# Gate pieces moved from the first steps of one attention into the last steps of the one before it

## The chip, the cores and the metric

The kernel runs on one core of one Trainium2 chip. The metric is the device time of one execution, in microseconds; the number given is the median of several runs.

## The reference

Two transformer layers in sequence, on 512 rows of 1024 columns, all in 32-bit floats. The change lies in the second layer, whose mixing part is, cut to what matters:

```python
h = rms_norm(x, g_mix)
proj = h @ w_in
sb_q, sb_k, sb_v, d_q, d_k, d_v, m_q = jnp.split(proj, IN_SPLITS, axis=-1)
y_sb = stick_breaking_attention(...) @ w_o_sb      # 8 heads, no softmax: a reverse cumulative sum
y_dil = dilated_mixture(...) @ w_o_dil             # 3 groups of 4 heads, dilations 1, 4, 16
y_mem = memory_attention(...) @ w_o_mem            # 4 heads over 256 memory rows
gates = jax.nn.sigmoid(h @ w_gate + b_gate)        # 3 x 1024 columns
merged = gates[0] * y_sb + gates[1] * y_dil + gates[2] * y_mem
x = x + merged @ w_out
```

The product `h @ w_gate` needs only `h`, so it can be made at any time before `merged`.

## The kernel before

The kernel is one program of several blocks. In a block each of the five engines has its own instruction list, and waits for the others through semaphores, which count up; `e.wait_ge(*s(n))` waits for the n-th increment of s. At the end of a block all engines drain and meet at a barrier. Nothing of the next block starts before.

Two blocks matter here. The **first** (line 2260) is the stick-breaking attention with the projections of the dilated attention beside it. It is written as a pipeline over 41 steps: in step n, PE makes the scores of unit n (a head and a block of 128 queries), transposes the weights of unit n-5, multiplies the values of unit n-7, and so on; ACT (ScalarE) and DVE (VectorE) do their parts of other units (`pe_stick`, `act_stick`, `dve_stick`). The projections (`pe_jobs`) end with step 27.

The **second** (line 2461) is the dilated attention (`att_d`, 48 units, one a step) with the heads of the memory attention beside it. Its first steps prepare these: from step 2 to step 8 DVE squares, sums and scales six tiles of queries and keys (`dve_memory`; `dve_newton`, line 282, begins with the first operation of each norm's Newton step), with two small operations on ACT between (lines 274 and 276); PE transposes each from step 4 on (line 2382). The tiles come from DRAM, loaded by SP at the start of this block (line 2466), behind a load of 1.5 MB of gate weights (`load_early`, line 1590).

The **gate pieces** are filler for PE. Of the product `h @ w_gate` (transposed, 24 units of 128 gate columns and all 512 rows), 12 units are made early, in 96 pieces. A piece (`pe_early(e, p)`, lines 1603 to 1615) is a unit s = p // 8 and a slice k = p % 8 of the inner dimension, in three matmuls of 128x512, since a 32-bit product is made of a high and a low part of each side. For unit s:

- ACT rounds the weights to the high part (`act_early`, line 1596), DVE subtracts to get the low part (`dve_early`, line 1601). The two are called a split below. Unit s needs its split before its first piece.
- The result goes to bank `EB[s]` of PSUM: 4, 5, 4, 7, 6, 7 for units 0 to 5.
- When the eighth piece is done, DVE (first block, line 2306) or ACT (`act_early_out`, line 2421) copies the bank to a buffer, and SP stores it to DRAM (`store_early`, line 1624).

In the first block the splits of units 0 to 4 stand at steps 27, 29, 31, 35 and 39 (`EARLY_AT`). PE makes two pieces in each of the steps 28 to 39, 24 in all, so units 0, 1 and 2. DVE copies them out at steps 32, 36 and 40. In the second block the list `FILL` says how many pieces PE makes in each step, ahead of that step's attention. Two tables follow from it: `SPLITS` (the step of each further split: one step after unit s-3 has ended) and `OUTS` (the step of ACT's copy: one step after the unit has ended). In the order of a step, ACT makes its split and its copy first, then its part of the memory heads and of the attention; DVE makes its split last.

Of the kernel before, what the change touches and what calls it, by code (L numbers as in the profile page):

```python
# [176 lines left out]
def r(a):  # L177
    return a.bitcast(F32R)


def span(k, w=128):
    return slice(w * k, w * k + w)


def program(nc, d, out, sizes):
    ctx = ExitStack()
    with ctx:
# [29 lines left out]
        def sems(names, new=False):  # L217
            return [sem(n, new) for n in names.split()]
# [981 lines left out]
        with ExitStack() as c0:  # L1200
# [359 lines left out]
            def load_job(e, t):  # L1560

                if t >= 26:
                    e.wait_ge(*j_mm(4 * (t - 26) + 4))
                e.dma_start(JW[t % 2][0][:, 0:sizes[t]], w_src(t)).then_inc(*w_in[t % NS].up(16))
# [24 lines left out]
            def load_early(e, g):  # L1589
                e.dma_start(ER[g % 2][0].rearrange("p k n -> p (k n)"), w_src(31 + 2 * g)).then_inc(*er_in[g % 2].up(16))  # L1590
# [12 lines left out]
            def pe_early(e, p):  # L1603
                s, k = divmod(p, 8)
                g, b = divmod(s, 3)
                bk, hi, lo = bank[EB[s]], EH[:, k, span(b)], ER[g % 2][1][:, k, span(b)]
                if k == 0:
                    e.wait_ge(*e_lo(s + 1))
                    if early_prior(s) >= 0:
                        e.wait_ge(*e_out(early_prior(s) + 1))  # L1610
                e.matmul(bk, r(lo), r(HTh[:, k, :]), start=k == 0, stop=False)
                e.matmul(bk, r(hi), r(HTl[:, k, :]), start=False, stop=False)
                i = e.matmul(bk, r(hi), r(HTh[:, k, :]), start=False, stop=k == 7)
                if k == 7:
                    i.then_inc(*e_mm.up(1))
# [351 lines left out]
        with ExitStack() as c0:  # L1967
# [34 lines left out]
            with ExitStack() as c1:  # L2002
# [21 lines left out]
                j_sq, j_out, j_var, j_root, j_norm, j_turn, j_keep, j_cols, j_odd = sems("j_sq j_out j_var j_root j_norm j_turn j_keep j_cols j_odd")  # L2024
# [231 lines left out]
                        e.tensor_scalar(va_[n % 2], ss, 1.0 / 64, EPS, ALU.mult, ALU.add).then_inc(*j_var.up(1))  # L2256

                EARLY_AT = (27, 29, 31, 35, 39)

                with nc.Block() as block:  # L2260
                    @block.sync
                    def _(e):
                        e.wait_ge(*mq_done(64))
                        for t in range(26, 31):
                            load_job(e, t)
                        e.wait_ge(*j_turn(16))
                        e.wait_ge(*j_var(16))
                        e.dma_start(BD, d["bd"]).then_inc(*bd_in.up(16))
                        e.wait_ge(*j_mm(24))
                        load_early(e, 0)  # L2270
                        e.wait_ge(*j_mm(28))
                        load_early(e, 1)
                        for s in range(3):
                            store_early(e, s)

                    @block.tensor
                    def _(e):
                        for step in range(41):
                            pe_stick(e, step)
                            pe_jobs(e, step)  # L2280
                            if 28 <= step < 40:
                                if step in (28, 32):
                                    e.wait_ge(*j_out(27 + (step - 28) // 4))
                                for p in range(2 * step - 56, 2 * step - 54):
                                    pe_early(e, p)

                    @block.scalar
                    def _(e):
                        exp_and_ln(e)
                        for step in range(42):  # L2290
                            if step in EARLY_AT:
                                act_early(e, EARLY_AT.index(step))
                            act_stick(e, step)
                            act_jobs(e, step)

                    @block.vector
                    def _(e):
                        for step in range(41):
                            dve_stick(e, step)
                            dve_jobs(e, step)  # L2300
                            if step in EARLY_AT:
                                dve_early(e, EARLY_AT.index(step))
                            if step in (32, 36, 40):
                                s = (step - 32) // 4
                                wait_early_out(e, s)
                                e.tensor_copy(ZG[s % 2], bank[EB[s]]).then_inc(*e_out.up(1))

# [3 lines left out]
            with ExitStack() as c1:  # L2311
# [51 lines left out]
                STEPS = att_d.steps()  # L2363

                FILL = [2] * 10 + [1] * 4 + ([0] * 2 + [1] * 8) * 2 + [0] * 6 + [1] * (STEPS - 40)
                filled = [24 + int(x) for x in np.cumsum([0] + FILL)]
                ended = lambda s: next((step for step in range(STEPS) if filled[step + 1] >= 8 * s + 8), STEPS)
                split_at = lambda s: max(0, ended(s - 3) + 1) if s > 5 else 0  # L2370
                SPLITS, OUTS = {split_at(s): s for s in range(5, 12)}, {ended(s) + 1: s for s in range(3, 12) if ended(s) < STEPS}
# [1152 lines left out]
```

## Time and profile before

| what | before |
|---|---|
| runs, us | 2824.06, 2825.64, 2825.81 (median 2825.64) |
| profiled execution, us | 2824.89 |
| its span, us | 2823.1 |
| busy us: PE, DVE, ACT, POOL | 2753.9, 2015.8, 1380.0, 441.9 |
| mean granted clock of TensorE | 0.992 |
| first block, us from the span's start | about 1060 to 1249 |
| second block | about 1250 to 1385 |

Times in the rows are microseconds from the start of the span. PE is TensorE's matmuls, PEld its weight loads, DVE is VectorE, ACT ScalarE, SP the engine that issues most DMAs; a q behind the name is the engine's queue (drains, semaphores, DMA issues). A bracket behind a row gives the idle time before it and what ended it. Ends of matmuls are modelled; from start to start is the surer measure. Granted clock 1.00 is 2.4 GHz, 0.50 is 1.2 GHz.

### The profile page before, as it was taken

The page shows a single profiled execution, that of the slowest core. Times are in us where ns is not written, and L with a number is a line of the kernel's source. Part 1 is how long each engine was busy: PE and PEld are TensorE (multiplying, and loading weights), DVE is VectorE, ACT ScalarE, POOL GpSimd, SP SyncE. Part 2 cuts the span into 40 slices and gives each one's busy share as a digit, 9 for nine tenths or more (in the row PEclk, how much of TensorE's full clock was granted, in tenths as well). Part 3 has the DMA queues.
Part 4 walks back from the last instruction along what each step waited for, and adds up shares of the span by engine and source line. Part 5 has one row for each costly group of instructions (what it writes and reads, how often), then busy time and mean ns, then how long its engine had stood idle before and what let it go on. Part 6 is the DMA issues. An engine that isn't in the chain of part 4 may idle for free. (4 is left out here: it accounts for less than half of the span.)

```text
span 2823.1 us, 36694 instructions
## 1 busy us (share of the span) xinstructions
PE 2753.9 (98%) x13927; PEld 2344.3 (83%) x13927; DVE 2015.8 (71%) x3290; ACT 1380.0 (49%) x2203; POOL 441.9 (16%) x294
## 2 busy tenths in 40 slices
PE   8989999999999899989999999999999999999999
PEld 6756888688888689968788889999999988888887
DVE  5575533688888616775654787788788868888886
ACT  4336522477777516665432433466667733333332
POOL 0000000010100000000000000222224424454442
PEclk9999999999999999999999999999999999999999
DMA  5000262667776521121242424777889989999996
GB/s 197 29 24 1 90 172 99 269 238 303 279 305 254 221 81 64 68 85 39 96 141 96 160 97 144 236 261 279 295 280 337 361 313 390 385 388 395 391 387 258
DMA packets 166623, 600.48 MB, mean 213 GB/s; under 512 B 16048, under 2 KB 87472, under 8 KB 138288
## 3 DMA queue, kind: packets, MB, share of 16 engines
q1 hardware_dynamic: 107696, 436.08, 42.3%
q0 software_dynamic: 41472, 138.45, 13.1%
q10 hardware_dynamic: 17280, 23.60, 2.3%
q8 instruction: 112, 1.84, 0.3%
q14 instruction: 63, 0.52, 0.1%
HBM read 563.96 MB, written 71.86 MB: 225 GB/s over the span
## 5 line engine op out<-in xcount | busy, mean ns | idle before, releaser
L2893 POOL DMA_INDIRECT RG<-in_un,EI x128 | 200.9, 1569 | 1155.7 <-DVE EI L3163 824.6
L2893 POOL DMA_INDIRECT RG<-in_vn,EI x128 | 198.2, 1548 | 276.5 <-DVE X L2907 253.4
L3288 PE MATMUL bank<-VH,GL 128*128 128x512 f32 x768 | 208.0, 392 | 0.4 <-DVE GL L2959 0.4
L3284 PE MATMUL bank<-VH,GH 128*128 128x512 f32 x768 | 207.9, 392 | 0.0
L2907 DVE SCALAR_TENSOR_TENSOR X<-RG,DG,X 128x1024 f32<-128x1024 f32 x128 | 164.1, 1282 | 53.3 <-DMA RG<-in_vn,EI 50.9
L2874 PE MATMUL bank<-HTl,UHe 128*128 128x384 f32 x512 | 175.2, 342 | 0.0
L2874 PE MATMUL bank<-HTl,UH1r 128*128 128x384 f32 x512 | 174.6, 341 | 0.0
L3288 PEld LDWEIGHTS bank<-VH,GL 128*128 128x128 f32 x768 | 144.1, 188 | 33.3 <-DVE GL L2959 0.9
L2875 PE MATMUL bank<-HTh,UHe 128*128 128x384 f32 x512 | 171.4, 335 | 0.0
L2875 PE MATMUL bank<-HTh,UH1r 128*128 128x384 f32 x512 | 171.3, 335 | 0.0
L3284 PEld LDWEIGHTS bank<-VH,GH 128*128 128x128 f32 x768 | 144.2, 188 | 32.5
L2904 DVE CUSTOM_DVE_ANT_0 RG<-RG,HR 128x1024 f32<-128x1024 f32 x128 | 156.5, 1222 | 16.2 <-DMA RG<-in_un,EI 15.4
L2966 ACT ACTIVATE VH<-VR 128x2048 fp32r<-128x2048 f32 x64 | 119.6, 1909 | 93.3 <-DMA VR<-in_vn 93.3
L3262 ACT ACTIVATE GA<-bank 128x384 f32<-128x384 f32 x120 | 58.3, 486 | 164.3 <-PE bank L2878 161.4
L3200 ACT ACTIVATE OAB<-OAB,IA 128x128 f32<-128x128 f32 x384 | 122.2, 392 | 16.9 <-DVE OAB L3193 16.0
L3193 DVE TENSOR_TENSOR OAB<-C,IA 128x1024 f32<-128x1024 f32 x96 | 116.9, 1221 | 1.6 <-PE bank L3208 1.5
L3292 PE MATMUL bank<-VR0r,GH 128*128 128x512 f32 x384 | 105.3, 396 | 0.2 <-DVE VR0r L2971 0.2
L3292 PE MATMUL bank<-VR1r,GH 128*128 128x512 f32 x384 | 102.9, 390 | 0.2 <-DVE VR1r L2971 0.2
L3208 PE MATMUL bank<-OAB 128*128 128x128 f32 x768 | 98.4, 275 | 2.0 <-ACT OAB L3200 2.0
L3208 PEld LDWEIGHTS bank<-OAB 128*128 128x128 f32 x768 | 96.4, 191 | 2.4 <-ACT OAB L3200 2.4
L2874 PEld LDWEIGHTS bank<-HTl,UHe 128*128 128x128 f32 x512 | 96.3, 188 | 0.8 <-DVE HTl L3440 0.5
L2874 PEld LDWEIGHTS bank<-HTl,UH1r 128*128 128x128 f32 x512 | 96.3, 188 | 0.2
(749 smaller groups left out, 7589.5 us busy)
## 6 DMA issues: line engine op xcount, KB each, us to landing
VR<-in_vn SPq DMA_DIRECT2D x32, 2048.0 KB
UP<-in_wup SPq DMA_DIRECT2D x22, 2048.0 KB, 7.6
UR<-in_u SPq DMA_DIRECT2D x42, 1024.0 KB
DN<-in_wdn SPq DMA_DIRECT2D x32, 1024.0 KB, 7.4
wspill<-VR SPq DMA_DIRECT2D x12, 2048.0 KB
aspill<-GA ACTq DMA_DIRECT2D x120, 192.0 KB
URew<-in_u SPq DMA_DIRECT2D x22, 1024.0 KB
W<-in_weights SPq DMA_DIRECT2D x10, 2048.0 KB, 9.3
```

Source lines behind the costliest of these rows:

```text
L2874: e.matmul(bk, r(hi[:, k, :]), r(HL_[:, k, 0:NT3]), start=k == 0, stop=False)
L2875: e.matmul(bk, r(hi[:, k, :]), r(HH_[:, k, 0:NT3]), start=False, stop=False)
L2893: e.indirect_dma_start(RG[q % RR], None, d["un" if what == "u" else "vn"][:, :], off).then_inc(*row_in[q % RR].up(16))
L2904: e.tensor_tensor_reduce(RG[q % RR], RG[q % RR], HR3, 1.0, 0.0, ALU.mult, ALU.add, DT[:, s:s + 1]).then_inc(*r_used.up(1))
L2907: e.scalar_tensor_tensor(X[:, 3, :], RG[q % RR], DG[:, s:s + 1], X[:, 3, :], ALU.mult, ALU.add).then_inc(*r_used.up(1))
L2966: e.activation(r(VH[n % 3]), VR[g % 2][0][:, :, span(n % 2, 512)], ACT.Copy).then_inc(*v_hi.up(1))
L3193: e.tensor_tensor(OAB[n % 3], cc("iota").unsqueeze(1).unsqueeze(1).to_broadcast(to), IA[:, 0:2, span(n, 4)].unsqueeze(3).to_broadcast(to), ...
L3200: i = e.activation(OB[n % 3][:, j, :], OB[n % 3][:, j, :], ACT.Copy, scale=IA[:, 2, t:t + 1])
L3208: i = e.matmul(bank[2 + n % 3][:, span(j)], OA[n % 3][:, j, :], OB[n % 3][:, j, :], start=True, stop=True)
L3284: e.matmul(bk, r(gh[:, a, t]), r(vh[:, a, :]), start=g == 0 and a == 0, stop=False)
L3288: e.matmul(bk, r(gl[:, a, t]), r(vh[:, a, :]), start=False, stop=False)
L3292: i = e.matmul(bk, r(gh[:, a, t]), r(vl[:, a, :]), start=False, stop=g == 31 and a == 3)
```

## The change

The first block's pieces are now given by a table: two in each of the steps 28 to 35, three in each of 36 to 39, four in step 40; 32 in all, so units 0 to 3. DVE copies unit 2 out at step 39 where it was 40. In the second block the first eight steps have one piece each where they had two; from step 8 on it is as before, piece for piece. All 96 pieces are made, with the same banks.

```diff
--- before.py
+++ after.py
@@ -2256,6 +2256,7 @@
                         e.tensor_scalar(va_[n % 2], ss, 1.0 / 64, EPS, ALU.mult, ALU.add).then_inc(*j_var.up(1))
 
                 EARLY_AT = (27, 29, 31, 35, 39)
+                PIECES = [int(x) for x in np.cumsum([0] * 29 + [2] * 8 + [3] * 4 + [4])]
 
                 with nc.Block() as block:
                     @block.sync
@@ -2278,11 +2279,10 @@
                         for step in range(41):
                             pe_stick(e, step)
                             pe_jobs(e, step)
-                            if 28 <= step < 40:
-                                if step in (28, 32):
-                                    e.wait_ge(*j_out(27 + (step - 28) // 4))
-                                for p in range(2 * step - 56, 2 * step - 54):
-                                    pe_early(e, p)
+                            if step in (28, 32):
+                                e.wait_ge(*j_out(27 + (step - 28) // 4))
+                            for p in range(PIECES[step], PIECES[step + 1]):
+                                pe_early(e, p)
 
                     @block.scalar
                     def _(e):
@@ -2300,8 +2300,8 @@
                             dve_jobs(e, step)
                             if step in EARLY_AT:
                                 dve_early(e, EARLY_AT.index(step))
-                            if step in (32, 36, 40):
-                                s = (step - 32) // 4
+                            if step in (32, 36, 39):
+                                s = (step - 31) // 4
                                 wait_early_out(e, s)
                                 e.tensor_copy(ZG[s % 2], bank[EB[s]]).then_inc(*e_out.up(1))
 
@@ -2364,8 +2364,8 @@
 
 
 
-                FILL = [2] * 10 + [1] * 4 + ([0] * 2 + [1] * 8) * 2 + [0] * 6 + [1] * (STEPS - 40)
-                filled = [24 + int(x) for x in np.cumsum([0] + FILL)]
+                FILL = [1] * 8 + [2] * 2 + [1] * 4 + ([0] * 2 + [1] * 8) * 2 + [0] * 6 + [1] * (STEPS - 40)
+                filled = [PIECES[-1] + int(x) for x in np.cumsum([0] + FILL)]
                 ended = lambda s: next((step for step in range(STEPS) if filled[step + 1] >= 8 * s + 8), STEPS)
                 split_at = lambda s: max(0, ended(s - 3) + 1) if s > 5 else 0
                 SPLITS, OUTS = {split_at(s): s for s in range(5, 12)}, {ended(s) + 1: s for s in range(3, 12) if ended(s) < STEPS}
```

`SPLITS` and `OUTS` are worked out from the new list. Since unit 3 now ends in the first block, the split of unit 6 and the copy of unit 3 move from step 4 to step 1; the others stay.

PE's list at the end of the first block and the start of the second, before (lines 1611 to 1613 are the three matmuls of a piece; bank 4 is unit 2, bank 7 unit 3; line 438 is a score of the dilated attention):

```order
L1611 MATMUL bank4<-Xr_49,ER0l_5188 128x512
L1612 MATMUL bank4<-HTr_50,EH_5191 128x512
L1613 MATMUL bank4<-Xr_49,EH_5191 128x512
L2260 UNCONDITIONAL_BRANCH
L2481 UNCONDITIONAL_BRANCH
L1611 MATMUL bank7<-Xr_49,ER1l_5190 128x512
L1612 MATMUL bank7<-HTr_50,EH_5191 128x512
L1613 MATMUL bank7<-Xr_49,EH_5191 128x512
L1611 MATMUL bank7<-Xr_49,ER1l_5190 128x512
L1612 MATMUL bank7<-HTr_50,EH_5191 128x512
L1613 MATMUL bank7<-Xr_49,EH_5191 128x512
L438 MATMUL bank0<-dkT,dqT 128x128
```

and with the change (bank 6 is unit 4):

```order
L1611 MATMUL bank7<-Xr_49,ER1l_5190 128x512
L1612 MATMUL bank7<-HTr_50,EH_5191 128x512
L1613 MATMUL bank7<-Xr_49,EH_5191 128x512
L2261 UNCONDITIONAL_BRANCH
L2481 UNCONDITIONAL_BRANCH
L1611 MATMUL bank6<-Xr_49,ER1l_5190 128x512
L1612 MATMUL bank6<-HTr_50,EH_5191 128x512
L1613 MATMUL bank6<-Xr_49,EH_5191 128x512
L438 MATMUL bank0<-dkT,dqT 128x128
L1611 MATMUL bank6<-Xr_49,ER1l_5190 128x512
L1612 MATMUL bank6<-HTr_50,EH_5191 128x512
L1613 MATMUL bank6<-Xr_49,EH_5191 128x512
```

The first block now ends with pieces of unit 3, and between its start and the first score the second block has one piece of unit 4 instead of two of unit 3.

ACT's list at the start of the second block, before (line 271 loads the activation table, 1596 is ACT's half of a split, 500 the exponential of an attention unit, 2421 a copy of a finished gate unit, 2396 a copy of a transposed memory tile):

```order
L271 ACT_TABLE_LOAD
L1596 ACTIVATE EH<-ER1w 128x8x128
L500 ACTIVATE Pd,RSd<-Pd,NMd 128x128
L274 ACTIVATE rtm<-vam 128x4
L276 ACTIVATE rtm<-rtm 128x4
L500 ACTIVATE Pd,RSd<-Pd,NMd 128x128
L274 ACTIVATE rtm<-vam 128x4
L276 ACTIVATE rtm<-rtm 128x4
L500 ACTIVATE Pd,RSd<-Pd,NMd 128x128
L1596 ACTIVATE EH<-ER0w 128x8x128
L2421 ACTIVATE ZG_5193<-bank 128x512
```

and with the change:

```order
L271 ACT_TABLE_LOAD
L1596 ACTIVATE EH<-ER1w 128x8x128
L1596 ACTIVATE EH<-ER0w 128x8x128
L2421 ACTIVATE ZG_5193<-bank 128x512
L500 ACTIVATE Pd,RSd<-Pd,NMd 128x128
L274 ACTIVATE rtm<-vam 128x4
L276 ACTIVATE rtm<-rtm 128x4
L500 ACTIVATE Pd,RSd<-Pd,NMd 128x128
L274 ACTIVATE rtm<-vam 128x4
L276 ACTIVATE rtm<-rtm 128x4
L500 ACTIVATE Pd,RSd<-Pd,NMd 128x128
```

The split of unit 6 (from ER0w) and the copy of unit 3 now stand ahead of the first exponential, where they stood behind the third. On DVE the other half of that split has moved in the same way, ahead of the first norm:

```order
 L470 ISA Pd,NMd<-bank,BD 128x128
 L470 ISA NMd 128x1
+L1601 TENSOR_TENSOR ER0l<-ER0w,EH 128x8x128
 L1991 TENSOR_TENSOR oTm<-oTm 128x512
 L1993 TENSOR_REDUCE ssm<-oTm 128x4
```

Line 470 is the reduction of an attention unit's scores, 1991 the first operation of a norm. SP's list is the same.

## Rows read from the trace of the kernel before

**Rows 1.** The page: its first line and the busy time of PE.

```profile
span 2823.1 us, 36694 instructions
...
PE 2753.9 (98%) x13927; PEld 2344.3 (83%) x13927; DVE 2015.8 (71%) x3290; ACT 1380.0 (49%) x2203; POOL 441.9 (16%) x294
```

**Rows 2.** Timeline of PE, end of the first block, start of the second (start us, us, what).

```profile
1245.46 0.40 PE L1611 MATMUL bank<-Xr,ER0l 128*128 128x512 f32 x1
...
1246.16 0.60 PE L2048 MATMUL bank<-C,oTm 128*128 128x128 f32 x4
...
1247.76 0.40 PE L1613 MATMUL bank<-Xr,EH 128*128 128x512 f32 x1
...
1249.68 0.47 PE L1611 MATMUL bank<-Xr,ER1l 128*128 128x512 f32 x1 [1.52 <-PEq L2260]
```

**Rows 3.** Windows: busy us of each engine, then granted clock, DMA share, GB/s.

```profile
1240.00:1248.20 8.20, 8.16 (x48) 6.63 (x46) 2.75 (x5) 3.58 (x5) 0.00 (x0) 1.00 0.09 34
```

**Rows 4.** Drains at the first block's end, line 2260 (durations ns, start us).

```profile
L2260 DVEq DRAIN  x1: 725/725/725, 1248.2 to 1248.2; - x1
...
L2260 SPq DRAIN  x1: 124/124/124, 1249.3 to 1249.3; - x1
```

**Rows 5.** The same for PE at the barrier of line 681.

```profile
L681 PEldq DRAIN  x1: 5332/5332/5332, 219.2 to 219.2; - x1
```

**Rows 6.** Timeline of PE behind that barrier.

```profile
224.84 1.10 PE L438 MATMUL bank<-kbT,qbT 128*128 128x512 f32 x2 [0.30 <-PEq L681]
```

**Rows 7.** Timeline of DVE, second block, steps 0 to 7.

```profile
1252.10 1.22 DVE L1601 TENSOR_TENSOR ER1l<-ER1w,EH 128x1024 fp32r<-128x1024 f32 x1 [3.21 <-ACT EH L1596]
...
1257.12 0.69 DVE L1991 TENSOR_TENSOR oTm<-oTm 128x512 f32<-128x512 f32 x1 [3.59 <-DMA oTm<-mqs]
...
1259.25 0.16 DVE L282 TENSOR_TENSOR thm<-rtm 128x4 f32<-128x4 f32 x1 [0.31 <-ACT rtm L276]
...
1262.96 0.16 DVE L282 TENSOR_TENSOR thm<-rtm 128x4 f32<-128x4 f32 x1 [0.31 <-ACT rtm L276]
...
1266.34 1.22 DVE L1601 TENSOR_TENSOR ER0l<-ER0w,EH 128x1024 fp32r<-128x1024 f32 x1
1267.47 0.15 DVE L282 TENSOR_TENSOR thm<-rtm 128x4 f32<-128x4 f32 x1
...
1271.18 0.16 DVE L282 TENSOR_TENSOR thm<-rtm 128x4 f32<-128x4 f32 x1
...
1278.01 0.29 DVE L461 COPY PTd<-bank 128x128 f32<-128x128 f32 x1
```

**Rows 8.** Timeline of SP's queue behind the barrier: the load for unit 6.

```profile
1249.63 0.33 SPq L1590 DMA_DIRECT2D ER0w<-in_weights  x1
```

**Rows 9.** DMA issues, window 1245 to 1262: KB, us to landing.

```profile
ER0w<-in_weights SPq DMA_DIRECT2D x1, 1536.0 KB, 6.8
```

**Rows 10.** Timeline of PE, second block: two waits, and a slow piece's start and follower.

```profile
1258.99 0.80 PE L438 MATMUL bank<-dkT,dqT 128*128 128x128 f32 x2 [3.53 <-DVE NMd L470]
...
1260.87 0.63 PE L1611 MATMUL bank<-Xr,ER1l 128*128 128x512 f32 x1
...
1262.15 0.41 PE L431 MATMUL bank<-C,Pd 128*128 128x128 f32 x1
...
1278.45 0.41 PE L431 MATMUL bank<-C,Pd 128*128 128x128 f32 x2 [0.60 <-DVE PTd L461]
```

**Rows 11.** Timeline of ACT, second block: a split's half and a copy.

```profile
1250.94 1.06 ACT L1596 ACTIVATE EH<-ER1w 128x1024 fp32r<-128x1024 f32 x1
...
1264.17 0.57 ACT L2421 ACTIVATE ZG<-bank 128x512 f32<-128x512 f32 x1
```

**Rows 12.** Windows, columns as in rows 3.

```profile
1234.00:1237.40 3.40, 2.02 (x15) 1.54 (x14) 3.21 (x4) 3.36 (x4) 0.00 (x0) 1.00 0.00 0
...
1259.00:1263.30 4.30, 4.16 (x12) 3.06 (x12) 3.40 (x12) 1.37 (x8) 0.00 (x0) 0.50 0.05 21
1263.30:1267.50 4.20, 3.44 (x14) 2.69 (x14) 3.92 (x11) 2.97 (x9) 0.00 (x0) 0.77 0.24 62
```

## The prediction

> **What bounds the kernel now.** I read the page first: TensorE (PE) is busy for 98% of a span of 2823.1 us [rows 1], so nearly every stretch is paced by PE, and the question is whether the places the change touches are among the exceptions. They are two blocks: the stick-breaking attention (steps 0 to 40) and, behind a barrier of all engines, the dilated attention with the memory heads.
>
> Next, PE's timeline at the end of the first block. From step 28 on each step carries two gate pieces, of three 128x512 matmuls each. There a piece costs 0.70 us from start to start (1245.46 to 1246.16 [rows 2]), and over steps 36 to 39 PE has no idle time: it is busy for 8.16 of 8.20 us [rows 3]. So those steps are PE's own, and whatever is added there is paid in full. Then comes the barrier: PE's last matmul ends at 1248.16 and the first of the next block starts at 1249.68, 1.52 us later [rows 2]. The rows of the drains say why. When PE is done, DVE is still copying unit 2 out of its bank until 1248.9; SP then issues the store of that copy and is drained at 1249.4 [rows 4], 0.3 us before PE's start. So it is the chain PE, DVE copy, SP store that ends the block. Where PE was itself the last to arrive, at the barrier of line 681 (drain of 5.33 us from 219.2, so to 224.5), it was idle for 0.30 us only [rows 5, 6].
>
> Third, DVE in the second block's first steps. At step 2 it wants the first memory queries from DMA and gets them at 1257.12, 7.49 us after SP's first issue at 1249.63 [rows 7, 8]. From there on it works through six norms, one a step. The starts of the first operation of the Newton step (line 282) are at 1259.25, 1262.96, 1267.47 and 1271.18, so 3.71, 4.51 and 3.71 us apart [rows 7], and two more follow in the last rhythm. The one longer step is the one with the split of unit 6 in it (1.22 us, line 1601). A period that stays at 3.71 us, at TensorE's half clock as at its full one, and whether the attention's tiles have 128 or 256 columns, has no PE in it: it is DVE's chain with ACT's two small operations between. PE waits for it: 3.53 us at 1258.99, and again at 1278.45 for the copy that DVE starts at 1278.01 [rows 7, 10]. Behind 1278.45 PE hardly waits any more; from step 8 on it is the bound again.
>
> **The change, part by part.**
>
> *Eight pieces more in the first block* (one each in steps 36 to 39, four in step 40). PE has no idle time to put them in: 8 x 0.70 = +5.60 us. No new wait: the weights of unit 3 are split in step 35 as before, and its bank 7 is free, since PE's product in step 38 already waits for the copy of the bank's last transposes.
>
> *The copy of unit 2 one step sooner.* Unit 2 now ends with the second piece of step 38; copy and store run beside the following pieces, six of them, 4.2 us against 0.69 us of copy and the 0.5 us to SP's drain. The barrier then waits for PE alone. I take the 0.30 us of the barrier where PE came last; the other bound is that the gap stays at 1.52. So 0.30 - 1.52 = -1.22 us, with 0 as the other end. The second block's first matmul starts 5.60 - 1.22 = 4.38 us later.
>
> *Eight pieces fewer in steps 0 to 7 of the second block.* 8 x 0.70 = 5.60 us of PE work go, at least. In steps 0 to 2 PE then reaches the wait for DVE sooner and waits longer. In steps 3 to 7 DVE's 3.71 us is the period, and PE is idle more. I cost it at 0. The cover is DVE's chain; were PE the pace in steps 3 to 7, five pieces would be worth 3.5 us, and that is the bound on this side.
>
> *Split and copy moved forward.* Since unit 3 now ends in the first block, ACT's split of unit 6 (line 1596) and its copy of unit 3 (line 2421) go from step 4 to step 1, and DVE's half of the split too. This adds a wait: ACT stands at step 1 until the weights have landed. SP issues them behind the barrier, as before, and they land 6.8 us later [rows 9]. Queued behind on ACT: the copy and the first exponential. Queued behind on DVE: step 2, the first norm. From the barrier: 6.8 landing + 1.06 ACT's half [rows 11] + 0.10 from its end to DVE's start (1252.00 to 1252.10 [rows 7, 11]) + 1.13 DVE's half (1266.34 to 1267.47 [rows 7]) = 9.09 us, where DVE started its norm at 7.49. That is +1.60 us. ACT's exponential comes after 6.8 + 1.06 + 0.57 [rows 11], at 8.4; PE asks for its result only behind its third scores, and these wait for a reduction that DVE makes behind the norm at 9.1, so it delays nothing. In return step 4 loses its split: 4.51 - 3.71 = -0.80 us. Net +0.80. Bounds: 0 (the weights land sooner and the queries are last again; then even -0.80) and +1.60 (step 4 does not get shorter).
>
> The Trainium skill has a formula for this landing (DMA: Bandwidth & Descriptors, "Anatomy of one DMA", there for transfers issued by GpSimd): 2.0 us and the bytes at 436 GB/s, which for 1.57 MB would be 5.6 us. By that the split would delay DVE by 1.2 us less and the sum would be 4.0; the trace's 6.8 us decides.
>
> *Sum:* 5.60 - 1.22 + 0 + 0.80 = **+5.2 us**. The profiled execution took 2824.89 us, its span and 1.8 us around it; with the sum 2830.1. It lies 0.75 below the median of the three runs (2825.64), to which I add the same: **2830.8 us**. Everything behind the second block sits behind further barriers and only shifts. About 0.2%, or 5.65 us, is what a measurement of this kernel can tell from no change; the forecast is just inside it.
>
> **The rivals.**
>
> *The clock stays low (slower).* PE's wait now spans some 6 us instead of 3.5. After the 3.5 us TensorE's granted clock fell to its lower level, 1.2 GHz, and stayed there throughout 1259.0 to 1263.3 though PE was busy for 4.16 of 4.30 us, and for some 1.9 of the next 4.20 us (mean 0.77) [rows 12]: 6.2 us in all. With one piece a step PE is less busy afterwards, and if it were still at 1.2 GHz when it becomes the bound in steps 8 and 9, another stretch of 6.2 us there would cost half of itself, 3.1 us: +8.3, 2833.9 us. It decides from the point where the low clock reaches beyond DVE's last norm. Against it: at the low clock a piece takes 1.28 us (1260.87 to 1262.15 [rows 10]), so PE is busy nearly all of the 3.71 us and should return to full speed; and a stretch with PE busy for 2.02 of 3.40 us kept a clock of 1.00 [rows 12]. The Trainium skill (TensorE: Matmul & The Clock Gate, Part 1) says that idling halves the clock and sustained work gives it back, and advises against gaps such as this change lengthens; by that rule too the low stretch begins during the wait, which DVE's chain covers. Chance 0.15.
>
> *The gap at the barrier does not close.* PE's gap was 1.52 us here, and no row shows it closing with a DMA store just finished. Then +6.4, 2832.0 us. For it: only one barrier shows the 0.30. Against it: its rows name DVE and SP as the late ones. Chance 0.14.
>
> *The removed pieces were on the path.* If PE is the pace in steps 3 to 7: 5.2 - 3.5 = +1.7, 2827.3 us. For it: PE is busy most of these steps, and waits there are short. Against it: the constant 3.71. Chance 0.15.
>
> *Something not seen makes it faster by over 0.2%.* All of PE's work is still there, and even with the last rival and the split at its lower end of -0.8 the sum is 5.60 - 1.22 - 3.5 - 0.8 = +0.1. Chance 0.06.
>
> **How the numbers follow.** My case has 0.50; its spread is about 1 us, so 0.38 of it lies within 0.2% and 0.12 above. Same: 0.38 + 0.15 = 0.53. Slower: 0.12 + 0.15 + 0.14 = 0.41. Faster: 0.06. The range reaches from a little under the third rival, 2826.0, to a little over the first, 2834.5; outside remain the 0.06 and the tails of both.
>
> **What would show each step.** In the changed profile: the last piece of the first block ends 5.6 us later with no idle time before it, and PE's idle time over the barrier is 0.3 us; DVE's first norm starts 9.1 us behind SP's first issue, released by ACT's split and not by DMA; PE's wait before the third scores grows from 3.5 to about 6 us; all five periods of line 282 are 3.7 us; the granted clock is 1.00 again before the last norm. I am wrong if these periods shrink (PE was the pace), if the low clock reaches into the steps with two pieces, or if the gap stays 1.5 us.

## The result, and the profile after

| | before | with the change |
|---|---|---|
| median of 12 runs, us | 2825.72 | 2829.93 |
| lowest to highest | 2821.02 to 2831.22 | 2827.48 to 2833.49 |
| ratio, 95% interval | | 1.0017 [1.0009, 1.0024] |
| span of the profiled execution | 2823.1 | 2830.3 |

The change makes the kernel slower by 0.17%, 4.8 us by the ratio and 4.2 by the medians; 5.2 was forecast. A second sample of the same kernel (experiment e12) gave 1.0016 [1.0008, 1.0025].

The page of the changed kernel hardly differs; compare [rows 1]. The number of instructions is the same, and PE has the same work (the share falls from 98% to 97%) in a longer span.

```profile
span 2830.3 us, 36694 instructions
...
PE 2755.3 (97%) x13927; PEld 2343.9 (83%) x13927; DVE 2016.1 (71%) x3290; ACT 1380.4 (49%) x2203; POOL 440.9 (16%) x294
```

The spans of the two profiles differ by 7.2 us, more than the kernels do. So first cut the time where it can be cut without doubt, at the barriers. In both profiles the barriers' semaphore rows give the time from one to the next; these are the blocks that matter here, with the ones around them:

| from barrier to barrier, us | before | after | after again (e12) |
|---|---|---|---|
| four blocks up to the first block | 1060.4 | 1062.0 | 1062.1 |
| first block | 189.2 | 193.5 | 193.5 |
| second block | 135.8 | 136.3 | 136.2 |
| third block | 173.8 | 173.8 | 175.4 |
| last block | 1263.8 | 1264.6 | 1264.3 |

The rows are printed to 0.1 us, so a difference can be 0.1 us off. In the 14 profiles of this study the first two blocks repeat to 0.2 us for the same instructions, with one exception (the first block of e1, below); the others wander by 2 to 4 us from profile to profile, whatever the kernel. So the change is +4.3 and +0.5 us, and the rest of the 7.2 is not its own.

**The end of the first block**, timeline of PE, to be laid beside [rows 2] and [rows 10]:

```profile
1241.67 0.48 PE L1611 MATMUL bank<-Xr,ER0l 128*128 128x512 f32 x1
...
1254.84 0.40 PE L1613 MATMUL bank<-Xr,EH 128*128 128x512 f32 x1
1255.56 0.47 PE L1611 MATMUL bank<-Xr,ER1l 128*128 128x512 f32 x1 [0.32 <-PEq L2261]
...
1259.47 0.62 PE L438 MATMUL bank<-dkT,W 128*128 128x128 f32 x2 [2.06 <-DVE NMd L470]
...
1266.22 0.80 PE L438 MATMUL bank<-dkT,dqT 128*128 128x128 f32 x2 [4.85 <-DVE NMd L470]
...
1288.34 0.60 PE L438 MATMUL bank<-dkT,dqT 128*128 128x256 f32 x2
```

The columns are start and duration in us, and in brackets the idle time before it and what ended it. From step 36's first piece (here 1241.67; before 1240.12) to the last matmul's end it takes 13.57 us where it took 8.04 us: +5.53 for eight pieces. There is no idle time in it, and the gap over the barrier is 0.32 us, where [rows 2] had 1.52. The drains say who came last, beside [rows 4]; DVE's copy is over at 1250.0, SP is drained at 1250.5, PE at 1255.3:

```profile
L2261 DVEq DRAIN  x1: 725/725/725, 1249.3 to 1249.3; - x1
L2261 SPq DRAIN  x1: 124/124/124, 1250.4 to 1250.4; - x1
...
L2261 PEldq DRAIN  x1: 4352/4352/4352, 1250.9 to 1250.9; - x1
```

**The start of the second block**, SP's first issue, its landing, and ACT, beside [rows 8], [rows 9] and [rows 11]:

```profile
1255.52 0.33 SPq L1590 DMA_DIRECT2D ER0w<-in_weights  x1
```

```profile
ER0w<-in_weights SPq DMA_DIRECT2D x1, 1536.0 KB, 6.6
```

```profile
1262.12 1.06 ACT L1596 ACTIVATE EH<-ER0w 128x1024 fp32r<-128x1024 f32 x1 [4.25 <-DMA ER0w<-in_weights]
1263.09 0.58 ACT L2421 ACTIVATE ZG<-bank 128x512 f32<-128x512 f32 x1
1263.56 0.39 ACT L500 ACTIVATE Pd<-Pd,NMd 128x128 f32<-128x128 f32 x1
```

ACT stands idle for 4.25 us for the weights, and the first exponential, behind split and copy, starts 8.04 us after SP's first issue.

**DVE's chain of norms**, beside [rows 7]:

```profile
1263.21 1.23 DVE L1601 TENSOR_TENSOR ER0l<-ER0w,EH 128x1024 fp32r<-128x1024 f32 x1 [3.80 <-ACT EH L1596]
1264.35 0.68 DVE L1991 TENSOR_TENSOR oTm<-oTm 128x512 f32<-128x512 f32 x1
...
1266.47 0.16 DVE L282 TENSOR_TENSOR thm<-rtm 128x4 f32<-128x4 f32 x1 [0.31 <-ACT rtm L276]
...
1270.18 0.16 DVE L282 TENSOR_TENSOR thm<-rtm 128x4 f32<-128x4 f32 x1 [0.31 <-ACT rtm L276]
...
1273.90 0.16 DVE L282 TENSOR_TENSOR thm<-rtm 128x4 f32<-128x4 f32 x1 [0.26 <-ACT rtm L276]
...
1277.61 0.16 DVE L282 TENSOR_TENSOR thm<-rtm 128x4 f32<-128x4 f32 x1
```

The first norm (1264.35) starts behind the split and not behind a DMA, 8.83 us after the issue; it was 7.49. The periods of line 282 are 3.71, 3.72 and 3.71 us: the 4.51 us one is gone. PE's ninth scores come at 1288.34, 32.82 us behind the issue at 1255.52; before it was 1281.90 behind 1249.63, 32.27 us (timeline of PE in the kernel before):

```profile
1281.90 0.60 PE L438 MATMUL bank<-dkT,dqT 128*128 128x256 f32 x2
```

So the way from DVE's first norm to the ninth scores takes 24.78 us before (1257.12 to 1281.90) and 23.99 us with the change (1264.35 to 1288.34): 0.79 us less, which is what the step lost with its split, and nothing for the eight pieces that are gone. The rest of the difference is the start of the chain, 8.83 against 7.49 us. From the third scores to the last of the block both profiles agree step by step to 0.05 us, but for the step that lost its split: 4.16 us before, 3.38 after.

**TensorE's clock**, windows (busy us of PE, PEld, DVE, ACT, POOL, then granted clock, DMA share, GB/s), beside [rows 3] and [rows 12]; first the whole low stretch of the kernel before, then the changed kernel:

```profile
1258.40:1265.20 6.80, 6.07 (x18) 4.78 (x19) 5.60 (x20) 3.48 (x11) 0.00 (x0) 0.50 0.11 45
```

```profile
1241.70:1255.20 13.50, 13.50 (x70) 11.07 (x68) 3.29 (x5) 3.43 (x5) 0.00 (x0) 1.00 0.11 40
...
1260.50:1266.20 5.70, 0.87 (x3) 0.14 (x1) 2.88 (x6) 2.12 (x5) 0.00 (x0) 0.50 0.77 303
1266.20:1273.20 7.00, 5.22 (x15) 3.60 (x15) 5.82 (x17) 2.08 (x9) 0.00 (x0) 0.50 0.06 16
1273.20:1277.50 4.30, 2.10 (x13) 1.79 (x13) 3.71 (x13) 1.98 (x8) 0.00 (x0) 0.98 0.33 75
```

The lower clock now lasts nearly 14 us (1259.7 to 1273.3) instead of nearly 7, and ends well ahead of the last norm at 1285. In the second profile of the same kernel (e12) it lasted 17 us, and the second block took no longer for it (136.2 us).

### The profile page after: what moved, and what is told of

Read it like the earlier page. It is cut to its first block and busy times, and to the rows that moved or that the text cites. A ratio compares the mean times of both kernels' runs of the same rounds, so it can differ in the third digit from the quotient of the medians.

```text
span 2830.3 us, 36694 instructions
## 1 busy us (share of the span) xinstructions
PE 2755.3 (97%) x13927; PEld 2343.9 (83%) x13927; DVE 2016.1 (71%) x3290; ACT 1380.4 (49%) x2203; POOL 440.9 (16%) x294
## 5 line engine op out<-in xcount | busy, mean ns | idle before, releaser
L2875 PEld LDWEIGHTS bank<-HTh,UHe 128*128 128x128 f32 x512 | 96.3, 188 | 0.2
```

The lines of the kernel that those rows point to most:

```text
L2875: e.matmul(bk, r(hi[:, k, :]), r(HH_[:, k, 0:NT3]), start=False, stop=False)
```

## The experiments

All edits are to the kernel named, and each kernel was timed beside the kernel before on the same chip. The ratios have intervals of about 0.09% to either side, 2.5 us, so that a difference of 1 us is read from the time between barriers, and only the sum from the ratio.

**e1: is it the early split that delays DVE?** In the changed kernel, split and copy back at step 4.

```diff
-split_at = lambda s: max(0, ended(s - 3) + 1) if s > 5 else 0
+split_at = lambda s: 4 if s == 6 else max(0, ended(s - 3) + 1) if s > 5 else 0
-OUTS = {ended(s) + 1: s for s in range(3, 12) if ended(s) < STEPS}
+OUTS = {(4 if s == 3 else ended(s) + 1): s for s in range(3, 12) if ended(s) < STEPS}
```

> The changed kernel, but unit 6's split and unit 3's copy stand at step 4 of the second block again. My theory (DVE's chain paces the steps 2 to 8, and the early split delays its start): DVE's first norm is released by the queries' DMA, 7.1 to 7.5 us behind SP's first issue instead of 8.8; the period of line 282 with the split in it is 4.5 us again, the others 3.7; PE's wait before the third scores is some 3.5 us instead of 4.85; from barrier to ninth scores the time is 0.4 to 0.7 us less than in the changed kernel (32.8 us). Rival (the delay is of the low clock or of the missing pieces, not of the split): the time from barrier to ninth scores stays at 32.8 us.

One execution, 2831.25 us; timeline of DVE:

```profile
1262.52 0.69 DVE L1991 TENSOR_TENSOR oTm<-oTm 128x512 f32<-128x512 f32 x1 [3.32 <-DMA oTm<-mqs]
...
1268.35 0.16 DVE L282 TENSOR_TENSOR thm<-rtm 128x4 f32<-128x4 f32 x1 [0.31 <-ACT rtm L276]
...
1271.72 1.22 DVE L1601 TENSOR_TENSOR ER0l<-ER0w,EH 128x1024 fp32r<-128x1024 f32 x1
1272.86 0.15 DVE L282 TENSOR_TENSOR thm<-rtm 128x4 f32<-128x4 f32 x1
```

The first norm waits for the DMA again, 7.21 us behind SP's issue at 1255.31; the period with the split in it (1268.35 to 1272.86) is 4.51 us; the second block takes 135.5 us instead of 136.3. The ninth scores come 0.85 us sooner than in the changed kernel, a little more than the 0.4 to 0.7 expected, since the queries landed sooner than in the kernel before (7.21 us and not 7.49). From the first norm to the ninth scores it takes 24.76 us, as before. The clock was low for as long as in the changed kernel, so it is the split that cost the half microsecond, not the clock.

This one profile is the exception among the first blocks: 195.0 us, 1.5 more than in the changed kernel, whose instructions it has there. A stretch of low clock fell just behind the barrier (the changed kernel has a clock of 1.00 there), and PE is busy in it:

```profile
1061.20:1064.50 3.30, 3.30 (x12) 3.30 (x12) 0.00 (x0) 0.38 (x1) 0.00 (x0) 0.50 0.01 2
```

**e2: is PE's work in the first eight steps free?** The kernel before, with all but the last matmul of units 3 and 4 left out: 46 of 48 matmuls of steps 0 to 7. Two of the twelve early gate units are then not what they should be.

```diff
 def pe_early(e, p):
...
+    if s in (3, 4) and k < 7:
+        return
...
+    if s in (3, 4):
+        e.matmul(bk, r(hi), r(HTh[:, k, :]), start=True, stop=True).then_inc(*e_mm.up(1))
+        return
```

> The kernel before, with units 3 and 4 of the gates left out but for one matmul each (46 of 48 matmuls, 10.7 us of PE work at full clock, of the first eight steps of the second block). My theory: PE's work in these steps is free, so leaving it out brings nothing: periods of line 282 stay 3.7 us (4.5 with the split), the ninth scores come within 0.3 us of the 32.3 us behind the barrier that they have in the kernel before, the total is within 1 us (ratio 0.9997 to 1.0004). Rival (the removed pieces were on the path): 3.5 us or more faster, ratio 0.9988 or less. Rival (low clock): PE is idle so much that the clock stays at 1.2 GHz into steps 8 and 9, and the total is 2 to 4 us longer, ratio 1.0007 to 1.0014.

Timeline of DVE, then windows:

```profile
1258.22 0.16 DVE L282 TENSOR_TENSOR thm<-rtm 128x4 f32<-128x4 f32 x1 [0.31 <-ACT rtm L276]
...
1261.94 0.16 DVE L282 TENSOR_TENSOR thm<-rtm 128x4 f32<-128x4 f32 x1 [0.31 <-ACT rtm L276]
...
1266.44 0.16 DVE L282 TENSOR_TENSOR thm<-rtm 128x4 f32<-128x4 f32 x1
...
1270.15 0.16 DVE L282 TENSOR_TENSOR thm<-rtm 128x4 f32<-128x4 f32 x1
```

```profile
1250.20:1277.50 27.30, 11.99 (x41) 9.21 (x42) 20.47 (x60) 10.45 (x33) 0.00 (x0) 0.50 0.38 138
1277.50:1284.00 6.50, 6.27 (x39) 5.40 (x40) 4.25 (x15) 5.03 (x14) 0.00 (x0) 0.98 0.11 40
```

3.72, 4.50 and 3.71 us: with nearly 11 us of PE work gone, the chain keeps its time. The second block took 135.7 us (before 135.8). This is the plainest sign that DVE's chain is the pace. The clock was low for 27 us, up to 1277.7, 3 us ahead of the ninth scores at 1280.86, and cost nothing either: from the first norm to the ninth scores it takes 24.76 us (before 24.78).

But the median was 2827.75 us, ratio 1.0018 [1.0009, 1.0027]: slower. The profile shows none of it in the two blocks; but the profiled execution took 2824.23 us, the second shortest of the twelve and less than the profiled one of the kernel before, so it can't show where the others lost their time. Two more runs asked why. **e9** has the same partial sums as e2 with all instructions in place (the last matmul of units 3 and 4 has `start=True`, so begins the sum anew):

```diff
-    e.matmul(bk, r(hi), r(HTl[:, k, :]), start=False, stop=False)
-    i = e.matmul(bk, r(hi), r(HTh[:, k, :]), start=False, stop=k == 7)
+    e.matmul(bk, r(hi), r(HTl[:, k, :]), start=False, stop=s in (3, 4) and k == 7)
+    i = e.matmul(bk, r(hi), r(HTh[:, k, :]), start=s in (3, 4) and k == 7, stop=k == 7)
```

> The kernel before, instruction for instruction, but the last matmul of units 3 and 4 begins its sum anew, so that these two units hold the same partial product as in e2 and only the data behind them differ. It asks why e2 took 4 us more in the median while its two blocks took none more. Theory A (the data: other gates, so other experts are chosen and other rows gathered later): the same ratio as e2, 1.0009 to 1.0027. Theory B (the missing matmuls, through the low clock or the layout of the program): 0.9995 to 1.0005.

It gave 1.0003 [0.9994, 1.0012], so the data alone hardly do it, though this interval still overlaps both of the other kernel's. **e10** is e2 once more:

> e2 once more (units 3 and 4 left out but for one matmul each), since its two blocks took no longer in the profile than before while its median was 4 us above, and e9 with the same data was not. If that was a sampling matter: ratio 0.9997 to 1.0007. If the missing work makes it slower: 1.0009 or more again, and a profile of a slow execution should show a low granted clock that reaches behind DVE's last norm, into steps 8 and later.

It gave 1.0011 [1.0002, 1.0019], with 189.1 and 135.5 us in the two blocks, and again a low clock of 27 us that ended with the last norm (at 1280.5). The expected low clock in steps 8 and later is not there; the profiled execution took 2826.91 us, again less than its sample's median (2827.97). The slowness repeats and no profile shows its place. The granted clocks of the single executions give a hint: their mean is 0.9879 and 0.9878 in the two samples, where the kernel before, timed beside them, had 0.9925 and 0.9923. That is some 26 us more at the lower level, and the second block, with 27 us instead of nearly 7, accounts for 20 of them. The 5 or 6 us left, at half price where PE is busy, would be an estimated 3 us of the 3 to 5. It is not shown; the cause stays open. What e2 was made for, the two blocks, is clear in both of its profiles.

**e3: does it matter where the pieces are taken from?** The changed kernel's 32 pieces in the first block, but taken out of steps 8 to 13, where PE is the bound.

```diff
-FILL = [1] * 8 + [2] * 2 + [1] * 4 + ([0] * 2 + [1] * 8) * 2 + [0] * 6 + [1] * (STEPS - 40)
+FILL = [2] * 8 + [0] * 6 + ([0] * 2 + [1] * 8) * 2 + [0] * 6 + [1] * (STEPS - 40)
```

> The changed kernel's first block (32 pieces), with two pieces in each of the second block's first eight steps as in the kernel before, and none in steps 8 to 13 (where before had two, two and four times one): the eight pieces are taken out where PE is the bound. My theory: 5.5 us dearer in the first block, 1.2 less at the barrier, 0.5 more for the early split, and up to 5.6 less in steps 8 to 13, as far as these steps have no other bound: total -0.7 to +1.5 us against before (ratio 0.9997 to 1.0005), so 4 to 5 us faster than the change. Rival (pieces are worth the same wherever they are taken out, and the change's cost comes from the block's end or from the split): the same total as the change, ratio 1.0017.

Ratio 1.0013 [1.0004, 1.0023], which alone would not part the two. The barriers do: first block 193.4 us, as in the change, second 133.1, which is 3.2 less than in the change and 2.7 less than before. The split of unit 6 stands at step 1 as in the change, but step 4 keeps one, that of unit 7, so the chain starts late (8.7 us) and saves nothing: 24.77 us to the ninth scores. From there to the fifteenth it took 10.94 us instead of 14.88: eight pieces of 0.70 gave 3.9 us and not 5.6, since with its filler gone PE waits for others (timeline of PE in e3):

```profile
1285.74 0.41 PE L431 MATMUL bank<-C,Pd 128*128 128x128 f32 x2 [1.65 <-issue]
...
1290.03 0.70 PE L438 MATMUL bank<-KV,mqT 128*128 128x256 f32 x2 [0.24 <-ACT PM L500]
```

So my figure for this place was too high by 1.7 us, and in sum the two blocks cost +1.5 us, the upper end of the -0.7 to +1.5 expected; the ratio came out above its forecast (0.9997 to 1.0005). The order of size holds: 0 for pieces out of DVE's steps, 3.9 us out of PE's.

**e4: what starts the chain?** The kernel before, with two query tiles loaded ahead of unit 6's weights.

```diff
 e.wait_ge(*e_mm(3))
+for tb in range(2):
+    e.dma_start(MS[tb], d["mqs"][span(tb), :]).then_inc(*mq_in[tb].up(16))
 load_early(e, 2)
-for tb in range(4):
+for tb in range(2, 4):
     e.dma_start(MS[tb], d["mqs"][span(tb), :]).then_inc(*mq_in[tb].up(16))
```

> The kernel before, with SP loading the first two query tiles ahead of unit 6's weights. My theory: DVE's chain of norms paces PE from the third scores to the ninth, and it starts when the first tile lands. It lands 2 to 2.6 us behind the barrier instead of 7.5, DVE is then ready 3.9 us behind the barrier (behind its split of unit 5 and the first reduction), so the chain starts 3.5 us sooner, PE's wait of 3.5 us before the third scores falls to nearly nothing, the clock stays at 2.4 GHz, the ninth scores come 3 to 3.6 us sooner and the total is 3 to 3.6 us shorter (ratio 0.9987 to 0.9990). Rival (PE is the pace once it does not wait): 0 to 1.5 us.

Timeline of DVE in e4:

```profile
1254.61 0.69 DVE L1991 TENSOR_TENSOR oTm<-oTm 128x512 f32<-128x512 f32 x1
...
1256.73 0.16 DVE L282 TENSOR_TENSOR thm<-rtm 128x4 f32<-128x4 f32 x1 [0.31 <-ACT rtm L276]
...
1260.44 0.16 DVE L282 TENSOR_TENSOR thm<-rtm 128x4 f32<-128x4 f32 x1 [0.31 <-ACT rtm L276]
...
1264.96 0.15 DVE L282 TENSOR_TENSOR thm<-rtm 128x4 f32<-128x4 f32 x1
```

The norm starts 3.82 us behind SP's first issue (1250.79) and waits for no DMA; the chain keeps its periods (3.71, 4.52); the ninth scores come 28.59 us behind the issue, 3.7 us sooner. Ratio 0.9991 [0.9982, 0.9999], 2.5 us. Of the 3.7 us the block kept 2.3 (133.6 us), since in this profile a stretch of low clock (1348.6 to 1352.0) fell in the steps without filler, 34 to 39, and the last three of these took 1.3 us longer than before. The rival's 0 to 1.5 us is out for the ninth scores.

**e5, e6, e7: the same reasons used for a better kernel.** e5 is e4 with the splits of units 6 and 7 at steps 9 and 11. e6 adds a piece in each of steps 2 to 5 and takes four out of steps 8 to 13. e7 adds the end of the first block as in the change, with two extra pieces only.

```diff
+split_at = lambda s: {6: 9, 7: 11}.get(s, max(0, ended(s - 3) + 1) if s > 5 else 0)      # e5, e6, e7
+FILL = [2, 2, 3, 3, 3, 3, 2, 2] + [1] * 4 + [0] * 2 + ([0] * 2 + ...                     # e6
+FILL = [2, 2, 3, 3, 3, 3, 2, 2] + [0] * 2 + [1] * 2 + [0] * 2 + ([0] * 2 + ...           # e7
+PIECES = [int(x) for x in np.cumsum([0] * 29 + [2] * 8 + [3, 3, 2, 1, 1])]               # e7, e8
-for p in range(2 * step - 56, 2 * step - 54):
+for p in range(PIECES[step], PIECES[step + 1]):                                          # e7, e8
-if step in (32, 36, 40):
+if step in (32, 36, 39):                                                                 # e7, e8
```

> The kernel before with the queries loaded first (as e4) and the splits of units 6 and 7 at steps 9 and 11 of the second block instead of 4 and 8. My theory (DVE's chain of norms is the pace up to the ninth scores): all five periods of line 282 are 3.7 us, the ninth scores come 0.8 us sooner than in e4 (28.6 us behind SP's first issue; e4 had 28.6 at 29.4 with its own split), total 4 to 5 us shorter than before, ratio 0.9983 to 0.9987. Rival (PE paces these steps once it does not wait): no gain over e4's 2.5 us.

> As e5, and four pieces more in steps 2 to 5 of the second block (three each), four fewer in steps 8 to 13. My theory: the four cost nothing where DVE's chain paces (period stays 3.7 to 3.8 us; PE's work of a step is then just under 3.7), and 2 to 2.8 us go from steps 8 to 13, where PE is the bound and e3 gained 3.9 us by eight pieces: total 6 to 7.5 us shorter than before, ratio 0.9973 to 0.9979. Rival (a piece costs its 0.7 us wherever it stands): the same as e5.

> As e6, and the first block's end as in the change, but with two pieces of unit 3 only (26 in all; unit 2 ends at step 38, its copy at step 39), taken out of steps 8 and 9. My theory: 1.4 us more before the barrier, 1.2 less at it (PE's gap 0.3 us), 0.7 to 1.4 less in steps 8 and 9: 0.5 to 1.2 us shorter than e6, ratio to before 0.9969 to 0.9977. Rival (the barrier's gap is not closed by two pieces, 1.8 us of PE work against 1.2 of copy and store): 0 to 1 us longer than e6.

> e7 once more, to narrow its interval. Its first two blocks together took 6.6 us less than before in the profile, and a third block with one more stretch at the low clock gave 1.6 us of it back. Expected ratio 0.9976 to 0.9986; if the low clock behind it is systematic 0.9982, else 0.9977.

DVE's chain in e5:

```profile
1252.91 0.69 DVE L1991 TENSOR_TENSOR oTm<-oTm 128x512 f32<-128x512 f32 x1
...
1255.04 0.16 DVE L282 TENSOR_TENSOR thm<-rtm 128x4 f32<-128x4 f32 x1 [0.31 <-ACT rtm L276]
...
1258.75 0.16 DVE L282 TENSOR_TENSOR thm<-rtm 128x4 f32<-128x4 f32 x1 [0.31 <-ACT rtm L276]
...
1262.47 0.16 DVE L282 TENSOR_TENSOR thm<-rtm 128x4 f32<-128x4 f32 x1 [0.26 <-ACT rtm L276]
...
1266.19 0.16 DVE L282 TENSOR_TENSOR thm<-rtm 128x4 f32<-128x4 f32 x1
```

All periods are 3.71 or 3.72 us now, and the ninth scores come 27.37 us behind the issue, 1.2 us sooner than in e4 (step 8 lost a split too). But the splits cost something where they went, at steps 9 and 11, behind the chain of norms: from the ninth scores to the fifteenth it takes 15.78 us, where it took 14.88. Of the 1.2 us, 0.3 are left.

| | first block | second block | third block | ratio to before |
|---|---|---|---|---|
| before | 189.2 | 135.8 | 173.8 | |
| e4 | 189.1 | 133.6 | 175.3 | 0.9991 [0.9982, 0.9999] |
| e5 | 189.1 | 131.9 | 177.0 | 0.9993 [0.9985, 1.0002] |
| e6 | 189.1 | 129.8 | 175.4 | 0.9984 [0.9974, 0.9994] |
| e7 | 189.3 | 129.1 | 175.4 | 0.9986 [0.9976, 0.9997] |
| e7 again (e11) | 189.3 | 129.1 | 173.8 | 0.9966 [0.9954, 0.9978] |

The second block shrinks at each step: 1.7 us from e4 to e5 (1.3 of them only because e4's profile had its stretch of low clock in steps 37 to 39; 0.3 are the splits'), 2.1 from e5 to e6 (three pieces a step did not stretch DVE's period: it is 3.72 in e6 too), 0.7 from e6 to e7, in whose first block the two pieces and the closed gap nearly cancel (+0.2). In all 6.6 us go from the two blocks (189.2 + 135.8 to 189.3 + 129.1). The ratios missed their forecasts: e5, e6 and the first e7 came out higher (0.9983 to 0.9987, 0.9973 to 0.9979 and 0.9969 to 0.9977 were forecast), e7's second sample lower (0.9976 to 0.9986). That e5's is no better than e4's fits the 0.3 us. The forecasts for e6 and e7 fit what the two blocks lost, 6.1 us (0.9978) and 6.6 us (0.9977), and these values lie within the measured intervals, so that the ratios alone can't say whether something was lost elsewhere. e7 beats both kernels in both of its samples, and the two samples' intervals hardly meet.

**e8: the barrier alone.** Kernel before, with e7's `PIECES`, copy of unit 2 at step 39, two pieces fewer in steps 8 and 9, splits kept where they were.

```diff
+FILL = [2] * 8 + [1] * 6 + ([0] * 2 + ...
+split_at = lambda s: {6: 4, 7: 8}.get(s, max(0, ended(s - 3) + 1) if s > 5 else 0)
```

> The kernel before with the barrier part of the change alone: 26 pieces in the first block (3, 3, 2, 1, 1 in steps 36 to 40), copy of unit 2 at step 39, and the two pieces taken out of steps 8 and 9 of the second block; splits of units 6 and 7 kept at steps 4 and 8, queries as before. My theory: first block 0.1 to 0.3 us longer (+1.4 for two pieces, -1.2 at the barrier, PE's gap 0.3 us), second block 0.7 to 1.4 shorter: 0.5 to 1.3 us shorter in all, which only the profile can show; ratio 0.9994 to 1.0001. Rival (the gap stays 1.5 us): first block 1.4 us longer.

Timeline of PE in e8, first matmul behind the barrier:

```profile
1247.36 0.47 PE L1611 MATMUL bank<-Xr,ER1l 128*128 128x512 f32 x1 [0.30 <-PEq L2261]
```

The gap closes with two pieces (1.4 us) behind unit 2's end as well as with the change's eight (5.6 us). First block 189.3 us, second 134.3; ratio 0.9997 [0.9988, 1.0005]. The second block's 1.6 us are a little more than the 0.7 to 1.4 expected: 0.4 of them came from queries that landed sooner (first norm 7.10 us behind the issue, not 7.49).

**e12: the change again.**

> The changed kernel once more beside these. My theory: +4.3 us from the first block and +0.5 from the second in every execution, ratio 1.0012 to 1.0022; first block 193.5 us from barrier to barrier, second 136.3, as in its first profile, and any other difference of a profile lies outside these two. Rival (the agreement of the first profile was luck): the second block differs from 136.3 by over 1 us.

1.0016 [1.0008, 1.0025], with 193.5 and 136.2 us: as the first time. From the first norm to the ninth scores it takes 23.99 us again.

## Why the prediction was right

- *Eight pieces at full price in the first block.* Forecast +5.60, measured +5.53 us, with PE busy for 13.50 of 13.50 us. Right.
- *The gap at the barrier closes.* Forecast -1.22 from one row of another barrier; measured 1.52 to 0.32, so -1.20. The rival that it stays open is out; e8 closes it too. The prediction counted six pieces (4.2 us) behind unit 2's end; they are eight, the whole of unit 3 (5.6 us), which makes the cover larger and changes no term.
- *Fewer pieces in steps 0 to 7 bring nothing.* Forecast 0, since the 3.71 us period did not move with the clock or the tile width. Right: after the change it is still 3.71, and e2 takes out twice as much PE work and it is still 3.71. From the first norm to the ninth scores it takes 24.76 to 24.79 us in the kernel before and in e1, e2 (both profiles), e3, e4 and e9, with two pieces a step, one, or hardly any PE work, and 23.99 us in both profiles of the change, without the split. The rival worth 3.5 us is out.
- *Split moved forward.* Forecast +1.60 for DVE's start and -0.80 at step 4; measured +1.34 (the weights landed after 6.6 us, not 6.8, and DVE began 0.03 us behind ACT's half, not 0.10) and -0.79 (4.51 to 3.72). Net +0.55 at the ninth scores against +0.80: right in kind, 0.25 us too high. e1 shows it by undoing it. The size hangs on when transfers land, which differs from profile to profile: the first norm came 7.10 to 7.49 us behind the issue wherever the queries were last, and 8.62 us behind it in e12, where the net is +0.35. The formula of the Trainium skill (DMA: Bandwidth & Descriptors, "Anatomy of one DMA"), which it gives for transfers issued by GpSimd, gave 5.6 us for the landing of this one, issued by SP; it took 6.6 us, so the measurement decides.
- *The clock.* It stayed low for about twice as long as before, which I had priced as a rival at +3.1 us if it reached steps 8 and 9. It ended 15 us ahead of the ninth scores, in e12 nearly 11. That it costs nothing so long as the chain paces, e2 shows with 27 us. The Trainium skill (TensorE: Matmul & The Clock Gate, Part 1) says that idling halves the clock and sustained work gives it back. This trace agrees on the first half: the level fell at 1258.4, within PE's wait of 3.53 us, in the kernel before, and at 1259.7, between two waits of 2.06 and 4.85 us, in the changed one. On the second half it adds that PE was busy for 5.22 of 7.00 us before the level rose. That the low stretch cost no time is what the runs here add.
- *Sum.* 4.3 + 0.5 = 4.8 us from the barriers, 4.8 by the ratio; forecast 5.2, range 0.4 to 8.9 above the median. That the ratio gives the same 4.8 is luck: its interval reaches 2 us to either side. What stands for the sum are its terms, each read between barriers.
- *One sign was read wrongly.* I had said that PE's wait before the third scores grows to about 6 us. It is 4.85, because the wait ahead of the second scores grew too, from 0.68 to 2.06 us: the two together are 6.9 us where they were 4.2. It changes no term.

## What to carry to other kernels

Filler for PE has a price by its place: full price where PE is the bound, nothing where another engine's chain sets the period, and in between where taking it out uncovers a wait (8 x 0.70 us gave 3.9). A period that stays the same to 0.01 us while PE's clock and work change is the surest sign of such a chain, and then what to shorten is the chain's start and its links (here a load queued behind a larger one, and a split that could wait), not PE's work. An operation that a planner moves together with its unit brings its wait along: look at what it stands in front of. And what is moved out of one engine's chain has a price where it goes (e5: 1.2 us gained, 0.9 given back).

## What the runs showed that I had not expected

A kernel with 46 matmuls fewer was slower twice, 1.0018 and 1.0011, with both blocks around the missing work unchanged in their profiles. Its cause is open.

Most of the spread between executions of one kernel goes with the mean granted clock of TensorE. Of the 35 executions of the kernel before that were timed beside e5, e6, e7 and e9, seven had a mean clock of 0.991 and took 2828.6 us on average, ten had 0.992 and took 2826.2, nine had 0.993 and took 2822.8, five had 0.994 and took 2821.1.

The third block takes 173.8, 175.4 or 177.0 us (to 0.1 us, in 14 profiles) though nothing in it was edited, and this follows TensorE's clock. Windows of the kernel before (173.8 us), and of e5 (177.0 us), in the same stretch behind the barrier at 1385.4 and 1380.9:

```profile
1396.00:1403.00 7.00, 7.00 (x22) 5.01 (x21) 5.84 (x8) 2.58 (x1) 0.00 (x0) 0.76 0.00 0
1403.00:1410.00 7.00, 7.00 (x27) 4.54 (x26) 2.75 (x4) 0.98 (x1) 0.00 (x0) 1.00 0.01 2
```

```profile
1391.00:1398.00 7.00, 7.00 (x15) 4.05 (x14) 6.31 (x8) 2.05 (x1) 0.00 (x0) 0.52 0.00 0
1398.00:1405.00 7.00, 7.00 (x26) 4.56 (x25) 1.72 (x3) 0.00 (x0) 0.00 (x0) 0.99 0.00 0
1405.00:1412.00 7.00, 7.00 (x25) 5.58 (x24) 5.78 (x6) 5.86 (x8) 0.00 (x0) 0.76 0.35 109
```

PE is busy throughout in both, yet the granted clock falls to 1.2 GHz for some 3.5 us in the one (0.76 of 7 us) and for 7 and then 3.5 us in the other: 1.6 us more for each additional 3.5 us at the lower level. It falls on kernels with the same program in different ways: 173.8 us in the changed kernel's first profile and 175.4 in its second, 175.4 in e7 and 173.8 in e11. So a profile of this kernel can carry 1.6 or 3.2 us that have nothing to do with the edit.

What PE did before the level fell is no ordinary work. Timeline of PE, first in the kernel before, then in e5:

```profile
1393.34 3.70 PE L2611 MATMUL bank<-dqT,C 4*128 4x512 f32 x8
```

```profile
1388.80 4.78 PE L2613 MATMUL bank<-dqT,C 4*128 4x512 f32 x8
```

These are eight matmuls with operands of 4 partitions instead of 128. Four more follow 6 to 9 us later. In all 14 profiles every low stretch of this block begins during one of these two groups or up to 1.3 us behind it, some profiles behind the first alone, some behind the second alone, some behind both. So they, and not the wide matmuls, are the likely occasion. No kernel without them was run, so this is not shown. An earlier end of the second block, which e4 to e8 have in common, is not what it takes: e1 and e12, whose second block ends late, have two stretches as well, and e11 has one only.
